# First modulation on unsplit weights in column-tiled pairs, last down pieces and final chain by token halves: a one-core diffusion backbone layer on Trainium2

## The chip, the cores and the metric

The kernel runs on one core of one Trainium2 chip, as one launch. The metric is the device time of that launch in microseconds, from the first to the last instruction of the core and what lies around them. Lower is better.

## What is computed

One layer of a hybrid backbone on 256 tokens `x` and 256 context tokens `ctx`, width 2048, all in fp32. Cut to what matters here:

```python
sh1, sc1, gt1, sh2, sc2, gt2 = adaln(c, w_mod[l], b_mod[l])            # silu(c) @ w_mod + b_mod, 6 rows of 2048
csh1, csc1, cgt1, csh2, csc2, cgt2 = adaln(c_ctx, w_mod[l], b_mod[l])  # of these only csh1 and csc1 are needed
hx = modulate(rms_norm(x, g_mix[l]), sh1, sc1)                         # xn * (1 + scale) + shift
hc = modulate(rms_norm(ctx, g_mix[l]), csh1, csc1)
x_pool, x_u, x_v, x_lru, x_lg, x_q, x_k, x_val = jnp.split(hx @ w_in[l], N_IN_SLICES, axis=-1)
...
x_mixed = x + gt1 * merge_branches(hx, [y_pool, y_sgu, y_lru, y_na], w_branch[l], w_gate[l], w_out[l])
hx2 = modulate(rms_norm(x_mixed, g_ffn[l]), sh2, sc2)
x = x_mixed + gt2 * swiglu(hx2, w_ffn_gate[l], w_ffn_up[l], w_ffn_down[l])
return rms_norm(x, g_final)
```

The "first modulation" is sh1 and sc1, for `c` and for `c_ctx`: two vectors of 2048 against 2048 x 4096 of `w_mod`, 32 MB of weights that are read once. The tokens can't be projected before they are modulated.

## The kernel before

**Pieces.** Every weight matrix comes in pieces of two 128x512 tiles side by side (128x1024 fp32, 512 KB). SyncE issues their transfers into a ring of raw slots. Nearly every piece is split on the chip for two fast matmul passes: ScalarE writes a rounded copy HI (in fp32r), VectorE the rest LO = raw - HI, and TensorE multiplies HI and LO apart. Three matmuls (high by high, high by low, low by high) stand for one in full precision; `rows3` and `piece_rows` (L1276 to L1278) and `piece` issue them. HI and LO have four slots each; ScalarE refills a slot when TensorE has counted the semaphore `used` for the piece that was there. A piece with 256 tokens costs TensorE 12 matmuls of 512 columns, one with 512 tokens (tokens and context) 24.

**The start.** The list `START` has 72 pieces: 64 of the first modulation, as ("mod", q, j), and 8 of the keys' weights, as ("keys", q, j). Quarter q makes 512 columns of shift (j 0 to 7) and of scale (j 8 to 15); j also picks 256 of the 2048 rows. A modulation piece takes four matmuls with the vectors as the stationary operand, 4 columns wide (high and low parts of both vectors, in `SC`), each with HI or LO as its 512 moving columns (L1353). 12 of the 64 pieces, the set `WHOLE`, are left unsplit and take two plain fp32 matmuls with `SCF` (L1347); the chip runs each of these as two instructions. When a quarter is summed up, ScalarE copies its 4 rows out of PSUM (`MROW`, L471), TensorE turns them into columns (`MOD_TURN`, L1244), VectorE adds the bias and makes the factor `A1` (`mod1_columns`), and the four slices of tokens that belong to it are modulated (ScalarE the context, L439; VectorE the tokens, L777) and split into high and low (L446, L782). Then the keys pieces ("keys", q, 0 and 1) can run (`piece`, L1248 to L1250). All of this is one order written by hand: after each piece of `START` each engine runs its `start(p)`. The four rows of tokens and context (`XTOK`, 1 MB each) are sent between the first modulation pieces. Slots of the start are eight (`raw_first`): a raw slot is free when its LO is made, or for an unsplit piece when TensorE has used it.

**The middle** (the other projections, the branches, the gates, the output projection, the feed-forward) is in the same code in both versions. TensorE goes through its pieces in program order; the remaining modulations are summed on VectorE beside it.

**The end.** `ENDING` lists the last 16 pieces of the down projection by column quarter n. Quarter 3 is last: pieces 28 to 31 of the ending, both token halves (PSUM banks 6 and 7) side by side in each piece. `final_down(3)` on VectorE then does 256 tokens in one operation of 128x1024 each: times the gate, plus the residual, times the norm's factor. ScalarE squares and sums, loads the table for the square root, VectorE takes the reciprocal, and both scale the rows, half of the columns at a time, before SyncE stores them in four transfers of 512 KB.

The two lines that say what a modulation piece costs TensorE:

```python
i = mm(ps[0:4, 4 + j // 8, :], SC[:, 2 * (j % 8) + t, :], part[:, p % RING, t * BW:(t + 1) * BW],
       start=j % 8 + t + w == 0, stop=j % 8 + t + w == 9, skip_group_check=True)
```

Of the kernel before, what the change touches and what calls it, by code (L numbers as in the profile page):

```python
# [24 lines left out]
F32R = mybir.dt.float32r  # L25
# [4 lines left out]
P = 128  # L30
D = 2048
# [24 lines left out]
START = [("mod", q, j) for q in range(2) for j in range(16)]  # L56
for _i in range(4):
    START += [("keys", _i // 2, _i % 2)] + [("mod", 2 + _i // 2, _i % 2 * 8 + j) for j in range(8)]
START += [("keys", q, j) for q in (2, 3) for j in range(2)]
STARTED = len(START)  # L60
START_RING = 8

WHOLE = {p for p, (kind, q, j) in enumerate(START) if kind == "mod" and q < 2 and j % 8 in (2, 4, 6)}

MOD_TURN = [23, START.index(("mod", 1, 15)) + 4, START.index(("mod", 2, 15)) + 4, STARTED - 4]

def after_turn(q, steps):

    return STARTED - 1 if q == 3 else MOD_TURN[q] + 3 + steps

WIN0 = STARTED - 8
# [57 lines left out]
def build(nc, x, c, ctx, c_ctx, w_mod, b_mod, g_mix, g_ffn, g_final, w_in, w_pool, pool_scale,  # L133
# [3 lines left out]
    with ctxs:  # L137
# [15 lines left out]
        SC = sb("SC", [P, KT, 4], F32R)  # L153
# [35 lines left out]
        MROW = BR[0:4, 8192:9216]  # L189
        RAWX = BR[:, 10240:12288].rearrange("p (s e) -> p s e", s=2)  # L190
        CROW = BR[0:2 * KT, 12288:12416]
# [34 lines left out]
        def raw_first(p):  # L226
            r = p % START_RING
            extra = (RAWX[:, 0, :], RAWX[:, 1, :], MR.rearrange("p s e -> p (s e)"), ACCM.rearrange("p s e -> p (s e)"))
            return RAW[:, r, :] if r < RING else extra[r - RING]
# [8 lines left out]
        landed_first = [sem(f"first_landed{s}") for s in range(START_RING)]  # L238
# [24 lines left out]
        def _(sp):  # L263
            def first_piece(p, view, q, col):
                last = p - START_RING
                if last in WHOLE:
                    sp.wait_ge(used, last + 1 + 4)
                elif last >= 0:
                    sp.wait_ge(lo_done, last + 1 + 4)
                sp.dma_start(raw_first(p).rearrange("p (t n) -> p t n", t=2),  # L270
                             view[:, q, :, col:col + BW]).then_inc(landed_first[p % START_RING], 16)
# [10 lines left out]
            for p, (kind, q, j) in enumerate(START):  # L282
                if kind == "mod":
                    first_piece(p, v_mod, j % 8, j // 8 * D + q * BW)
                else:
                    first_piece(p, v_in, 2 * q + j, S_K * BW)
                if p in (3, 5, 7, 9):
                    k = (p - 3) // 2
                    sp.dma_start(XTOK[:, k, :], tokens[k]).then_inc(s(f"tokens{k}"), 16)
            for n, sl in enumerate(WIN_ORDER):  # L290
                if n == 0:
                    continue
                for j in range(8):
                    piece(WIN0 + 8 * n + j, j, v_in, j, sl * BW)
# [38 lines left out]
            for half in range(2):  # L333
                for t in range(2):

                    sp.wait_ge(s(f"rows_done{t}"), half + 1)
                    cols = slice(half * D // 2, (half + 1) * D // 2)
                    sp.dma_start(out[0, t * P:(t + 1) * P, cols].rearrange("p (n e) -> p n e", n=2),
                                 OTOK[:, 2 * half:2 * half + 2, t, :]).then_inc(s(f"stored{t}"), 16)
            for t in range(2):  # L340
                sp.wait_ge(s(f"stored{t}"), 32)
# [68 lines left out]
        def _(act):  # L410
            own = Own(act, own_a)

            def first_high(p):

                act.wait_ge(landed_first[p % START_RING], 16 * (p // START_RING + 1))
                act.wait_ge(used, p + 1)
                act.activation(HI[:, p % RING, :], raw_first(p), ACT.Copy).then_inc(hi_done, 2 if p + 1 in WHOLE else 1)  # L417

            def high(base4, j):

                act.wait_ge(landed[j % RING], base4 * 16 + 16 * (j // 4 + 1 - STARTED // RING))
# [7 lines left out]
            act.wait_ge(s("siluc"), 1)  # L429
            act.activation(SC[:, :, 0:2], SCF[:, :, :].rearrange("p w k -> p k w"), ACT.Copy).then_inc(s("sc_hi"), 1)  # L430

            def input_context(q):

                act.wait_ge(s("mod1_ready"), q // 2 + 1)
# [13 lines left out]
            def start(p):  # L448

                if p in (7, 9, 11, 13):  # L450

                    k = (p - 7) // 2
                    act.wait_ge(s(f"tokens{k}"), 16)
                    act.activation(ATT[:, k * D:(k + 1) * D], XTOK[:, k, :], ACT.Square, accum_out=ST[:, k:k + 1])\
                        .then_inc(s("ssq"), 1)
                if p == 13:
                    act.wait_ge(s("ssq"), 4)
                    act.activation(ST[:, 4:8], ST[:, 0:4], ACT.Sqrt, bias=EPSC[:, 0:1], scale=1.0 / D).then_inc(s("rms"), 1)
                if 20 <= p < 28:
                    b = 2 * (p - 20)  # L460
                    act.wait_ge(s("x_turned"), b + 1)
                    act.activation(XT[:, b // 8, b % 4 * 4:b % 4 * 4 + 4, b // 4 % 2 * P:b // 4 % 2 * P + P],
                                   ps[:, b % 4, :].rearrange("p (k t) -> p k t", k=4), ACT.Copy).then_inc(s("xt_act"), 1)
                for q in range(4):
                    for part in range(2):
                        done = START.index(("mod", q, 8 * part + 7))
                        if p == done + 4:
                            act.wait_ge(used, done + 1 + 4)
                            if q:
                                act.wait_ge(s("mod1_turned"), q)  # L470
                            act.activation(MROW[:, part * BW:(part + 1) * BW], ps[0:4, 4 + part, :], ACT.Copy)\  # L471
                                .then_inc(s("mrow"), 1)
                for q in range(4):
                    for t in range(2):
                        if p == after_turn(q, 2 + t):
                            input_context(2 * q + t)
                        if p == after_turn(q, 3 + t):
                            input_high(2 * q + t)

            for p in range(STARTED):  # L480
                if p not in WHOLE:
                    first_high(p)
                start(p)
# [177 lines left out]
            high(FFN0 // 4, 1)  # L661
            square(3)
            act.activation(ST[:, 62:63], EPSC[:, 0:1], ACT.Sqrt)
# [47 lines left out]
            for i in range(8):  # L711
                act.wait_ge(s("xf_new"), i // 2 + 1)
# [15 lines left out]
        def _(dve):  # L728
# [56 lines left out]
            def start(p):  # L785
# [20 lines left out]
                for q in range(4):  # L806
                    if p == after_turn(q, 1):
                        mod1_columns(q)
# [859 lines left out]
```

## Time and profile before

| | |
|---|---|
| median of 3 runs | 1722.19 us (1720.59 to 1722.87) |
| the profiled execution | 1720.87 us |
| its span, first to last instruction | 1719.2 us |
| TensorE busy | 1657.7 us (96%), 7647 matmul instructions |
| VectorE, ScalarE busy | 1150.8 us (67%), 783.6 us (46%) |
| HBM read | 385.30 MB, 226 GB/s over the span |
| mean granted TensorE clock | 0.988 of full speed |

The span is what the rows below are cut from. 1.7 us of the profiled execution lie outside it, and it is 1.3 us below the median. A busy TensorE in the profile is one with an instruction in flight: matmuls overlap, so the distance from start to start says what one costs, not its own length.

### The profile page before, as it was taken

The numbers are of one execution on the slowest core, as the hardware profiler recorded it, in microseconds if no ns is written. First come the engines' busy times: TensorE is split into PE (matmuls) and PEld (weight loads), VectorE is DVE, ScalarE is ACT, GpSimd is POOL, SyncE is SP. The second block draws the span as 40 slices with busy tenths as digits, with TensorE's granted clock in tenths as the row PEclk, the third lists the DMA queues.
The fourth block names the chain that finished last, engine by engine and source line by source line (L and its number), as shares of the span: only waits on it lengthen the run. The fifth ranks groups of instructions, "written<-read, shape, count | busy, mean of one in ns | idle before, by whom it ended". The sixth has DMA issues, their size and how long they took to land.

```text
span 1719.2 us, 22469 instructions
## 1 busy us (share of the span) xinstructions
PE 1657.7 (96%) x7647; PEld 1328.7 (77%) x7647; DVE 1150.8 (67%) x1260; ACT 783.6 (46%) x850; POOL 158.7 (9%) x294
## 2 busy tenths in 40 slices
PE   5899999999989999999999899999999999999996
PEld 1447888897668888878878688888888888888875
DVE  2785345688778888877866658667666555465485
ACT  4584323446764444434444644434444444434433
POOL 1002011110002312313100002011010000000000
PEclk9999999999999999999999899999999999999998
DMA  9887455765448979989855468778786666666552
GB/s 360 290 307 224 123 184 172 232 212 180 135 150 302 326 262 324 338 286 326 289 182 184 128 190 283 235 250 272 236 285 186 193 189 190 188 192 192 161 187 107
DMA packets 183799, 389.10 MB, mean 226 GB/s; under 512 B 14304, under 2 KB 14544, under 8 KB 182848
## 3 DMA queue, kind: packets, MB, share of 16 engines
q1 hardware_dynamic: 160720, 312.63, 56.2%
q0 software_dynamic: 23024, 75.74, 12.8%
q8 instruction: 34, 0.56, 0.1%
q14 instruction: 21, 0.17, 0.0%
HBM read 385.30 MB, written 3.01 MB: 226 GB/s over the span
## 4 chain that ended last, share of the span: by engine, by line
PE 85%; DVE 7%; ACT 4%; DMA 3%; issue 1%; SPq 0%; ACTq 0%; DVEq 0%
PE ps L1276 23%; PE ps L1278 23%; PE ps L1277 23%; PE ps L1248 3%; PE ps L1250 3%; PE ps L1249 3%; DMA RAW<-in_w_mod 2%; PE ps L1244 2%; DVE LO L734 2%; ACT HI L424 1%; DVE LO L738 1%; DMA RAW<-in_w_branch 1%; PE ps L1353 1%; PE ps L1347 1%; ACT HI L417 0%
## 5 line engine op out<-in xcount | busy, mean ns | idle before, releaser
L738 DVE TENSOR_TENSOR LO<-RAW,HI 128x1024 fp32r<-128x1024 f32 x512 | 625.5, 1224 | 459.4 <-ACT HI L424 457.1
L424 ACT ACTIVATE HI<-RAW 128x1024 fp32r<-128x1024 f32 x512 | 541.9, 1060 | 801.9 <-PE ps L1278 679.8
L1276 PE MATMUL ps<-HI,H 128*128 128x512 f32 x1920 | 755.8, 394 | 16.3 <-DVE LO L738 10.8
L1278 PE MATMUL ps<-HI,H 128*128 128x512 f32 x1920 | 749.7, 390 | 0.0
L1277 PE MATMUL ps<-LO,H 128*128 128x512 f32 x1920 | 749.5, 390 | 0.0
L1276 PEld LDWEIGHTS ps<-HI,H 128*128 128x128 f32 x1920 | 361.7, 188 | 97.5 <-DVE LO L738 13.3
L1278 PEld LDWEIGHTS ps<-HI,H 128*128 128x128 f32 x1920 | 361.7, 188 | 75.8
L1277 PEld LDWEIGHTS ps<-LO,H 128*128 128x128 f32 x1920 | 361.9, 188 | 75.1 <-issue 1.2
L388 POOL DMA_DIRECT2D BR<-in_w_mod x208 | 111.8, 538 | 749.8 <-DVE BR L842 330.6
L840 DVE SCALAR_TENSOR_TENSOR BR<-BR,SCF 128x512 f32<-128x512 f32 (+1 forms) x195 | 145.5, 746 | 3.4 <-DMA BR<-in_w_mod 1.9
L1248 PE MATMUL ps<-H,HI 128*128 128x256 f32 (+1 forms) x384 | 123.7, 322 | 3.7 <-DVE LO L734 3.4
L1249 PE MATMUL ps<-H,HI 128*128 128x256 f32 (+1 forms) x384 | 122.3, 319 | 0.0
L1250 PE MATMUL ps<-H,LO 128*128 128x256 f32 (+1 forms) x384 | 122.3, 318 | 0.0
L1248 PEld LDWEIGHTS ps<-H,HI 128*128 128x128 f32 x384 | 73.1, 190 | 11.1 <-issue 6.2
L1250 PEld LDWEIGHTS ps<-H,LO 128*128 128x128 f32 x384 | 73.1, 190 | 5.1
L1249 PEld LDWEIGHTS ps<-H,HI 128*128 128x128 f32 x384 | 73.2, 191 | 4.9
L1353 PE MATMUL ps<-HI,SC 128*4 128x512 f32 x104 | 43.7, 420 | 16.0 <-DVE LO L734 15.5
L734 DVE TENSOR_TENSOR LO<-RAW,HI 128x1024 fp32r<-128x1024 f32 x32 | 38.3, 1221 | 13.9 <-ACT HI L417 13.8
L388 POOL DMA_DIRECT2D MR<-in_w_mod x48 | 26.1, 546 | 210.3 <-DVE ACCM L840 145.7
L1146 DVE TENSOR_TENSOR ATT<-ps,ATT 128x1024 f32<-128x1024 f32 x36 | 43.8, 1216 | 0.0
L1353 PEld LDWEIGHTS ps<-HI,SC 128*4 128x4 f32 x104 | 9.0, 86 | 44.9 <-DVE LO L734 26.5
L1353 PE MATMUL ps<-LO,SC 128*4 128x512 f32 x104 | 43.5, 418 | 0.0
(250 smaller groups left out, 818.8 us busy)
## 6 DMA issues: line engine op xcount, KB each, us to landing
RAW<-in_w_gate SPq DMA_DIRECT2D x128, 512.0 KB, 4.7
BR<-in_w_mod POOLq DMA_DIRECT2D x208, 256.0 KB, 4.5
RAW<-in_w_ffn_gate SPq DMA_DIRECT2D x88, 512.0 KB, 3.8
RAW<-in_w_ffn_up SPq DMA_DIRECT2D x88, 512.0 KB, 3.9
RAW<-in_w_ffn_down SPq DMA_DIRECT2D x88, 512.0 KB, 3.7
RAW<-in_w_in SPq DMA_DIRECT2D x60, 512.0 KB, 4.3
RAW<-in_w_mod SPq DMA_DIRECT2D x32, 512.0 KB, 5.6
RAW<-in_w_branch SPq DMA_DIRECT2D x32, 512.0 KB, 5.0
```

Source lines behind the costliest of these rows:

```text
L388: pool.dma_start(slots[:, k % ring, :], w_mod[0, k * P:(k + 1) * P, bass.ds(2 * D + g * BW, BW)])\
L424: act.activation(HI[:, j % RING, :], RAW[:, j % RING, :], ACT.Copy).then_inc(hi_done, 1)
L734: tt(LO[:, p % RING, :], raw_first(p), HI[:, p % RING, :], ALU.subtract).then_inc(lo_done, 2 if p + 1 in WHOLE else 1)
L738: tt(LO[:, j % RING, :], RAW[:, j % RING, :], HI[:, j % RING, :], ALU.subtract).then_inc(lo_done, 1)
L840: i = stt(acc, src, SCF[:, 0, k:k + 1], acc, ALU.mult, ALU.add)
L1248: mm(o, wh, xh, start=first, stop=False, skip_group_check=True)
L1249: mm(o, wh, xl, start=False, stop=False, skip_group_check=True)
L1250: return mm(o, wl, xh, start=False, stop=last, skip_group_check=True)
L1276: mm(o, xh, wh, start=first and t == 0, stop=False, skip_group_check=True)
L1277: mm(o, xh, wl, start=False, stop=False, skip_group_check=True)
L1278: i = mm(o, xl, wh, start=False, stop=last and t == 1, skip_group_check=True)
L1353: i = mm(ps[0:4, 4 + j // 8, :], SC[:, 2 * (j % 8) + t, :], part[:, p % RING, t * BW:(t + 1) * BW], start=j % 8 + t + w == 0, stop=j % 8 + ...
```

## The change

- **The start.** Modulation pieces are no longer split. `SCP` holds for each 128 rows of `w_mod` the two vectors as plain fp32 columns, padded with zeros to 32. A pair of pieces is four fp32 matmuls, each to its own 32 PSUM partitions (`tile_position=(0, 32 * g)`), that is, in its own quarter of the array's columns; 32 pairs in all (`mod_pair`). The rows to be summed are then at partitions 0, 32, 64 and 96, and `mod1_turn` sums and turns them in one with `PICK`. Scale comes ahead of shift and is turned by itself (`part`). Modulation pieces have 7 raw slots (`MOD_RING`), free when TensorE has used them; keys pieces have raw slots 0 and 1 and are still split (`key_high`, `key_low`). The tokens are sent ahead of all pieces, the keys pieces among the modulation pieces of the same quarter, and TensorE mixes three steps of keys (9 matmuls) behind each of five pairs of the next quarter.
- **The end.** Quarter 3 of the down projection runs its four pieces for tokens 0 to 127 and then again for tokens 128 to 255 (`ending_half`); `last_rows(t)` does the chain for a half of the tokens, each with its own sum, root and reciprocal, and the stores are eight of 256 KB, the first half's ahead. The table for the root is loaded ahead of the last two squares.
- Ahead of the feed-forward, too, the root's table is loaded before the last squares.
- The merge of the branches works in token rows in both versions; no line of it is in the difference.

```diff
-            for p, (kind, q, j) in enumerate(START):
+            for k in range(4):
+                sp.dma_start(XTOK[:, k, :], tokens[k]).then_inc(s(f"tokens{k}"), 16)
+            for kind, q, j in START:
                 if kind == "mod":
-                    first_piece(p, v_mod, j % 8, j // 8 * D + q * BW)
+                    mod_piece(16 * q + j, v_mod, j % 8, (1 - j // 8) * D + q * BW)
                 else:
-                    first_piece(p, v_in, 2 * q + j, S_K * BW)
-                if p in (3, 5, 7, 9):
-                    k = (p - 3) // 2
-                    sp.dma_start(XTOK[:, k, :], tokens[k]).then_inc(s(f"tokens{k}"), 16)
+                    key_piece(2 * q + j)
...
+            def mod_piece(p, view, q, col):
+                if p >= MOD_RING:
+                    sp.wait_ge(s("mod1_used"), p - MOD_RING + 1)
...
+            def mod_pair(q, i):
+
+                part, p = i // 4, 16 * q + 2 * i
+                for p1 in (p, p + 1):
+                    pe.wait_ge(mod1_landed[p1 % MOD_RING], 16 * (p1 // MOD_RING + 1))
+                if q and i % 4 == 0:
+                    pe.wait_ge(s("mrow"), 2 * q - 1 + part)
+                for g in range(4):
+                    k = 4 * (i % 4) + g
+                    m = mm(ps[32 * g:32 * g + 32, 4 + part, :], SCP[:, k, :], mod_raw(p + g // 2)[:, g % 2 * BW:(g % 2 + 1) * BW],
+                           start=i % 4 == 0, stop=i % 4 == 3, skip_group_check=True, tile_position=(0, 32 * g))
+                m.then_inc(s("mod1_used"), 2)
...
+            pe.wait_ge(s("sc_set"), 1)
+            for i in range(8):
+                mod_pair(0, i)
+                if 1 <= i < 5:
+                    for b in range(4):
+                        rows_turn(4 * (i - 1) + b)
...
+            for q in range(1, 4):
+                work = keys(q - 1)
+                for i in range(8):
+                    mod_pair(q, i)
+                    if i == 0:
+                        mod1_turn(q - 1, 1)
+                    if i == 5:
+                        mod1_turn(q, 0)
+                    for _ in range(3 * (2 <= i < 7)):
+                        next(work)
+                next(work)
+            mod1_turn(3, 1)
+            for _ in keys(3):
+                pass
...
+            def ending_half(i, q):
...
+            pe.wait_ge(s("xf_new"), 2)
+            for q in range(2):
+                ending_half(6, q)
+                d = ending_half(7, q)
+                if q == 0:
+                    d.then_inc(s("last_half"), 1)
```

TensorE inside the start, before: the last matmul of a keys piece (L1250) and the first two pieces of modulation behind it.

```order
L1250 MATMUL ps<-H,LO 128x512
L1353 MATMUL ps<-HI,SC 4x512 [waits lo_done,mrow]
L1353 MATMUL ps<-LO,SC 4x512
L1353 MATMUL ps<-HI,SC 4x512
L1353 MATMUL ps<-LO,SC 4x512
L1353 MATMUL ps<-HI,SC 4x512 [waits lo_done]
L1353 MATMUL ps<-LO,SC 4x512
L1353 MATMUL ps<-HI,SC 4x512
L1353 MATMUL ps<-LO,SC 4x512
```

The same place now, in quarter 2: a pair (L1314), three of nine keys matmuls (L1233 to L1235 are `rows3`) and so on in turn.

```order
L1314 MATMUL ps<-BR 32x512 [waits mod1_landed2,mod1_landed1]
L1314 MATMUL ps<-BR 32x512 x3
L1233 MATMUL ps<-H,HI 128x512 [waits lo_done,h_lo]
L1234 MATMUL ps<-H,HI 128x512
L1235 MATMUL ps<-H,LO 128x512
L1233 MATMUL ps<-H,HI 128x512
L1234 MATMUL ps<-H,HI 128x512
L1235 MATMUL ps<-H,LO 128x512
L1233 MATMUL ps<-H,HI 128x512
L1234 MATMUL ps<-H,HI 128x512
L1235 MATMUL ps<-H,LO 128x512
L1314 MATMUL ps<-MR,BR 32x512 [waits mod1_landed4,mod1_landed3]
```

A pair of pieces was eight matmuls that waited for the split (`lo_done`); it is four that wait for the transfers alone, and keys come in between.

SyncE's queue at the start of the program, before (BR, MR and ACCM are raw slots beside RAW; BR<-in_ctx and BR<-in_x are the tokens):

```order
L270 DMA RAW<-in_w_mod 128x2x512 x4
L289 DMA BR<-in_ctx 128x2048
L270 DMA BR<-in_w_mod 128x2x512 x2
L289 DMA BR<-in_ctx 128x2048
L270 DMA MR<-in_w_mod 128x2x512
L270 DMA ACCM<-in_w_mod 128x2x512
L289 DMA BR<-in_x 128x2048
L270 DMA RAW<-in_w_mod 128x2x512 x2
L289 DMA BR<-in_x 128x2048
```

And now:

```order
L278 DMA BR<-in_ctx 128x2048 x2
L278 DMA BR<-in_x 128x2048 x2
L259 DMA BR<-in_w_mod 128x2x512 x3
L259 DMA MR<-in_w_mod 128x2x512
L259 DMA ACCM<-in_w_mod 128x2x512
L259 DMA RAW<-in_w_mod 128x2x512 x2
L259 DMA BR<-in_w_mod 128x2x512 x2
L265 DMA RAW<-in_w_in 128x2x512
```

The 4 MB of tokens moved ahead of the first modulation piece, and the first keys piece (in_w_in) from behind 32 modulation pieces to behind 9.

VectorE at the end of the program, before: `final_down(3)` for all tokens, the sum, the reciprocal, the scaling.

```order
L1193 TENSOR_TENSOR ATT<-ps,ACCM 128x1024 [waits piece_used]
L1194 TENSOR_TENSOR BR<-BR,ATT 128x2x512 [waits dve_own]
L1196 TENSOR_TENSOR ATT<-BR 128x1024 [waits xf_new]
L1226 TENSOR_REDUCE ST<-ST 128x2 [waits sqf]
L1228 MEMSET ST 128x1 [waits dve_own]
L1230 RECIPROCAL ST<-ST 128x2 [waits rms3]
L1235 TENSOR_SCALAR ATT<-ATT,ST 128x2x512 [waits y_new,rstd3]
L1235 TENSOR_SCALAR ATT<-ATT,ST 128x2x512
```

And now, the first of two halves (the second has the same rows, and waits for `piece_used` in place of `last_half`):

```order
L1206 TENSOR_TENSOR ATT<-ps,ACCM 128x512 [waits last_half]
L1207 TENSOR_TENSOR BR<-BR,ATT 128x512 [waits dve_own]
L1209 TENSOR_TENSOR ATT<-BR 128x512 [waits xf_new]
L1211 TENSOR_REDUCE ST<-ST 128x1 [waits sqf]
L1213 RECIPROCAL ST<-ST 128x1 [waits rms3]
L1217 TENSOR_SCALAR ATT<-ATT,ST 128x512 [waits y_new,rstd3]
```

Every operation has half the elements, and the first set waits for TensorE's middle of the last quarter, not for its end.

## Rows read from the trace of the kernel before

**Rows 1.** The page, chain that ended last: shares of the span by engine

```profile
PE 85%; DVE 7%; ACT 4%; DMA 3%; issue 1%; SPq 0%; ACTq 0%; DVEq 0%
```

**Rows 2.** Two stretches: busy of each engine, granted clock, DMA share, GB/s

```profile
10.00:50.00 40.00, 26.77 (x72) 5.98 (x71) 16.60 (x19) 21.29 (x23) 1.13 (x1) 0.88 1.03 388
...
84.90:114.70 29.80, 27.89 (x122) 14.23 (x121) 24.79 (x27) 22.92 (x26) 0.00 (x0) 1.00 0.89 305
```

**Rows 3.** Groups by line and shape, 0 to 150 us: count, busy us, mean ns

```profile
L1353 PE MATMUL ps<-HI,SC 128*4 128x512 f32 x104 | 43.7, 420 | 16.0 <-DVE LO L734 15.5
L734 DVE TENSOR_TENSOR LO<-RAW,HI 128x1024 fp32r<-128x1024 f32 x32 | 38.3, 1221 | 13.9 <-ACT HI L417 13.8
L1347 PE MATMUL ps<-RAW,SCF 128*2 128x512 f32 x16 | 8.1, 629 | 0.0
```

**Rows 4.** Timeline of TensorE in the start: start us, us, engine, line

```profile
51.90 1.03 PE L1244 MATMUL ps<-CST,BR 128*128 128x128 f32 x8
...
144.56 0.65 PE L1244 MATMUL ps<-CST,BR 4*128 4x4 f32 x8
...
145.95 0.39 PE L1248 MATMUL ps<-H,HI 128*128 128x512 f32 x1
...
161.60 0.39 PE L1276 MATMUL ps<-HI,H 128*128 128x512 f32 x1
```

**Rows 5.** The chain that ended last, in the start: start us, us, what

```profile
3.75 7.00 DMA RAW<-in_w_mod
...
52.94 1.81 PE ps L1347 x4
```

**Rows 6.** Groups by line and shape, 140 to 152 us, modulating quarter 3

```profile
L782 DVE TENSOR_TENSOR H<-ATT,H 128x1024 fp32r<-128x1024 f32 x2 | 2.5, 1225 | 1.7 <-ACT H L446 1.7
L439 ACT ACTIVATE ATT<-ATT,MC,A 128x256 f32<-128x256 f32 x4 | 2.2, 591 | 5.5 <-DVE A L766 5.5
L446 ACT ACTIVATE H<-ATT 128x1024 fp32r<-128x1024 f32 x2 | 2.1, 1062 | 0.1
L471 ACT ACTIVATE BR<-ps 4x512 f32<-4x512 f32 x1 | 0.6, 570 | 0.0
L765 DVE TENSOR_TENSOR MC<-ps,MC 128x16 f32<-128x16 f32 x1 | 0.2, 174 | 0.0
```

**Rows 7.** The chain at the first feed-forward piece: start us, us, what

```profile
963.28 1.21 PE ps L1569 x2
...
967.83 0.80 PE ps L1276
...
972.04 0.43 PE ps L1276
```

**Rows 8.** The chain at the end of the program: start us, us, what

```profile
1704.35 0.24 PE ps L1278
...
1704.61 1.24 DVE ATT L1193
...
1707.13 0.73 ACT ATT L715 x2
...
1710.60 1.15 ACT ATT L724
```

**Rows 9.** Timelines of VectorE and ScalarE at the end of the program

```profile
1694.88 1.23 DVE L738 TENSOR_TENSOR LO<-RAW,HI 128x1024 fp32r<-128x1024 f32 x1 [1.49 <-ACT HI L424]
...
1698.54 1.23 DVE L1196 TENSOR_TENSOR ATT<-BR 128x1024 f32<-128x1024 f32 x1
...
1710.60 1.42 DVE L1235 TENSOR_SCALAR ATT<-ATT,ST 128x1024 f32<-128x1024 f32 x2
```

**Rows 10.** Timeline of ScalarE, the root's table

```profile
1708.68 1.28 ACT L717 ACT_TABLE_LOAD   x1
```

**Rows 11.** Groups by line and shape, 940 to 1000 us: 128x512 on VectorE

```profile
L828 DVE TENSOR_TENSOR H<-ATT,H 128x512 fp32r<-128x512 f32 x8 | 5.5, 688 | 1.1 <-ACT H L674 1.1
```

**Rows 12.** Timeline of SyncE's queue: the four stores

```profile
1711.77 3.11 SPq L338 DMA_DIRECT2D out<-ATT  x4
```

More of the change, by code:

```diff
@@ L51 @@
 PITCH = 128
[L56 to L75, printed above, removed]
+START = []
+for _q in range(4):
+    for _j in range(16):
+        if _j in (9, 13):
+            START.append(("keys", _q, _j // 13))
+        START.append(("mod", _q, _j))
+MOD_RING = 7
+WIN0 = 0
 MIX0 = WIN0 + 8 * 8
@@ L480, in _ @@
[L480 to L483, printed above, removed]
+            for k in range(4):
+                act.wait_ge(s(f"tokens{k}"), 16)
+                act.activation(ATT[:, k * D:(k + 1) * D], XTOK[:, k, :], ACT.Square, accum_out=ST[:, k:k + 1])\
+                    .then_inc(s("ssq"), 1)
+            act.wait_ge(s("ssq"), 4)
+            act.activation(ST[:, 4:8], ST[:, 0:4], ACT.Sqrt, bias=EPSC[:, 0:1], scale=1.0 / D).then_inc(s("rms"), 1)
@@ L816, in _ @@
[L816 to L819 removed]
+            dve.wait_ge(s("rms"), 1)
+            own.did(dve.reciprocal(ST[:, 4:8], ST[:, 4:8])); own.wait()
+            for k in range(4):
+                ts(XTOK[:, k, :], XTOK[:, k, :], ST[:, 4 + k:5 + k], None, ALU.mult).then_inc(s("rows_scaled"), 1)
+            for b in range(1, 16, 2):
+                dve.wait_ge(s("x_turned"), b + 1)
+                dve.tensor_copy(XT[:, b // 8, b % 4 * 4:b % 4 * 4 + 4, b // 4 % 2 * P:b // 4 % 2 * P + P],
+                                ps[:, b % 4, :].rearrange("p (k t) -> p k t", k=4)).then_inc(s("xt_dve"), 1)
@@ new lines, in mod1_turn @@
+            def mod1_turn(q, part):
+                pe.wait_ge(s("mrow"), 2 * q + part + 1)
+                pe.wait_ge(s("params"), 1)
+                if q + part:
+                    pe.wait_ge(s("mod1_read"), 2 * q + part)
+                for k in range(4):
+                    c = 64 + 16 * q + 8 * part + 2 * k
+                    m = mm(ps[:, 7, c:c + 2], MROW[:, part * BW + k * P:part * BW + (k + 1) * P], PICK,
+                           start=True, stop=True, skip_group_check=True)
+                m.then_inc(s("mod1_turned"), 1)
@@ L1355, in _ @@
-                i.then_inc(used, 1)
-                start(p)
+                        for f in range(4):
+                            i = rows3(ps[:, f, :], *weights(p, t, f), *both(k0 + t), p + t == 0, p == 7 and t == 1)
+                            if t == 1 and f == 3:
+                                i.then_inc(used, 1)
+                            yield
+            pe.wait_ge(s("sc_set"), 1)
[5 more added lines that the diff above has]
+                if i == 5:
+                    params_turn()
+                if i == 6:
+                    mod1_turn(0, 0)
```

326 lines of the change are left out of this document (150 added, 176 removed).

## The prediction

> **What bounds the kernel now.** I read the chain that ended last first: 85% of it is TensorE [rows 1], so TensorE's program order sets the time, and only its waits or its own matmuls can give any back. Then the busy time by stretches, in the two places that the change touches. In the start there are two regimes. From 10 to 50 us the transfers are at their limit: the 16 DMA engines are full, 388 GB/s, and VectorE is busy for 16.60 of 40 us [rows 2]. After that they are not: from 84.90 to 114.70, one quarter of the start, they move 305 GB/s, TensorE is busy for 27.89 of 29.80 us and VectorE for 24.79, mostly with the splits of 1.22 us each [rows 2, 3]. TensorE comes to the first piece behind the start, the values' weights, at 161.60 us [rows 4]. At the end the reader is to see a serial tail: the last matmul ends at 1704.59 us, and nearly 15 us of VectorE, ScalarE and stores follow, to 1719.2 [rows 8, 12].
>
> **Units.** From the keys matmul at 145.95 to the one at 161.60 there are 69 starts, 0.227 us each [rows 4]. A keys piece has 24, 5.44 us, so the last two take 10.9 us. Two unsplit fp32 matmuls are four instructions in 1.81 us, so 0.905 us for one matmul and 0.4525 us for each of its two instructions [rows 5]. Eight transposed tiles of tokens take 1.0 us, 64 tiles 8 us; a turn of modulation rows takes 0.6 us [rows 4].
>
> **The start, before.** Each split piece of modulation is four matmuls of 0.23 us, 0.92 us; of the 64 pieces 52 are split (104 matmuls with HI, 104 with LO [rows 3]). So modulation costs TensorE 1.84 us for two pieces, and the splits of 52 pieces VectorE 63 us.
>
> **The start, after, by transfers.** 64 modulation and 8 keys pieces are 37.7 MB, the tokens 4.2 MB: 41.9 MB, all of it now queued without a wait for a split. At 388 GB/s [rows 2] that is 108.1 us, and from the first transfer at 3.75 us [rows 5] the last piece is in at 111.9 us. One piece is 1.35 us, a pair 2.70 us.
>
> **The start, after, by TensorE.** The trace has no matmul in a quarter of the columns, so a pair's cost is bounded from both sides. Below: the four matmuls run side by side, a pair in the time of one, 0.905 us. Above: one after another, 3.62 us. To either I add an allowance of 0.1 us for going from one kind of matmul to the other, which I chose. I take the low end: the four have their own columns, weights and PSUM partitions, and use the same rows of nothing but the input, so nothing that I can name in them is shared. What a quarter then costs TensorE: 8 pairs x 1.0 + 16 keys steps x 0.68 + 2 turns x 0.6 = 20.1 us, against 18 pieces x 1.35 = 24.3 us of transfers. The transfers set the pace, and seven raw slots (9.4 us of transfers) cover TensorE's lag, since a pair with nine keys matmuls takes 3.0 us against 2.70.
>
> Here a page of the skill bears on it. The Trainium skill, "TensorE: Matmul & The Clock Gate", Part 3, gives three column tiles of 32 columns and 512 moving columns a speed of 2.38 times one after another. By that, as an estimate, four tiles are some 3.2 times as fast, a pair costs 1.2 us and a quarter 21.7 us, and transfers still set the pace; no row of this case shows a tile.
>
> Behind the last landing at 111.9 us nothing is hidden: the pair 1.0, MROW's copy 0.57, the turn 0.6, the bias 0.17, two context slices 1.1, the high part 1.06, the low part 1.22 [rows 4, 6]: 5.7 us, then the two keys pieces, 10.9 us. In the old kernel this gap was covered by the keys pieces of quarter 2, which now run ahead of it. TensorE waits for some 3.5 us in it. What a wait like this does to the clock the trace shows ahead of the feed-forward: after the work at 963.28 (1.21 us) TensorE waits until 967.83, and the 11 matmuls from there to the one at 972.04 take 0.43 us each, the 1.2 GHz level, where the rest runs at 2.4 [rows 7]. That costs 11 x 0.2 = 2.2 us; I count it in full. So the values' weights start at 111.9 + 5.7 + 10.9 + 2.2 = 130.7 us where they started at 161.60: **30.9 us less**.
>
> What could spoil this in the first quarter: the tokens come first, so the first pair lands at 3.75 + 10 x 1.35 = 17.3 us, and TensorE idles until then. It has 8 pairs and 64 transposes to do in the first quarter, 16 us at the low price, while 16 pieces take 22 us, so it keeps up even at a clock of 0.88 [rows 2]. The squares, the root and the scaling of the tokens on ScalarE and VectorE lie in the same stretch, where neither has a split to do.
>
> **The middle.** The same instructions in the same order, fed through the same four slots: shifted, not changed. The table load that goes ahead of the last squares before the feed-forward takes 1.28 us [rows 10] off ScalarE's chain, but VectorE's copy of the last turned columns runs beside it there and ends as late. 0 us.
>
> **The end.** 48 matmuls of the last quarter stay 48. A half needs all four split pieces within 4 x 1.36 us. The last split ran from 1694.88 to 1696.1 [rows 9], the quarter starts at 1704.59 - 10.88 = 1693.7, and the half wants piece four at 1697.8: in time by 1.7 us. Tokens 0 to 127 are through at 1699.2. VectorE is at `final_down(2)` until 1699.8 [rows 9] and then does the first half's chain, three operations of 0.69 us [rows 11] and about 2.5 us more, by 1704.3, beside TensorE. At 1704.59 the second half: two operations of 0.69, the square 0.73 [rows 8], sum, root and reciprocal. These took 1710.60 - 1708.68 = 1.9 us with the table's 1.28 [rows 8, 10], so 0.66 without (the load starts when the squares end). One scaling, 0.4 us where 1024 columns take 0.71 [rows 9]. First store of the second half: 1704.59 + 1.40 + 0.73 + 0.66 + 0.4 = 1707.8, against 1711.77 [rows 12]. From that issue to the end it was 7.4 us for 2.10 MB, which at 388 GB/s is 5.4 us and 2.0 us fixed; for 1.05 MB it is 4.7. End at 1712.5: **6.7 us less**.
>
> **The sum.** 1719.2 - 30.9 - 6.7 = 1681.6 us span; the profiled execution lies 1.7 us above its span and the median 1.3 us above that: 1684.6 us. A measurement tells 0.2%, 3.4 us, from no change.
>
> **Rivals.**
>
 Against it: nothing. A quarter then costs TensorE 18.9 + 10.9 + 1.2 = 31.0 us and not the transfers' 24.3. The first quarter ends at 17.3 + 18.9 + 8 = 44.2, the fourth at 137.2, the start at 137.2 + 4.7 + 10.9 + 2.2 = 155.0: 6.6 us less. With the end's 6.7: 1705.9 span, 1709 us.
>
> *One after another* (the other side). A pair costs 3.72 us, a quarter 41.9 us. The first quarter ends at 17.3 + 29.8 + 8 = 55.1, the fourth at 180.8, the start at 198.6, which is 37 us later; with the end's 6.7 less, 1749.5 span, 1752 us. The start ends at 17.3 + 8 + 3 x 12.1 + 4.7 + 10.9 + 2.2 = 79.4 us plus 32 pairs, so it breaks even at a pair of 2.57 us and the whole kernel, with the end's 6.7 us, at 2.78; from there on it is slower. For it: no row shows any two matmuls side by side. Changing the array's tiling may also make TensorE run empty first, as the Trainium skill has it in "TensorEngine Tiling (Array Packing)", Key Properties; 0.2 us in each of 32 pairs would be 6 us where TensorE sets the pace.
>
> *Transfers don't hold the rate.* 388 GB/s is a row of 40 us. At 350 the start is 11.7 us longer, 1696 us.
>
> *The change does nothing* where the start gains what the clock and the gap behind the last landing take: needs a pair of 2.7 to 2.9 us, within 0.1 us of the break-even point.
>
> **Chances.** Side by side 0.53 (with a slower transfer rate in it 0.08), by halves 0.27, one after another or over 2.9 us a pair 0.16, in between with no change 0.04. The range leaves out the last two: from 1677 (400 GB/s, clock not lowered) to 1713 (by halves with 4 us of emptying). Faster 0.80, same 0.04, slower 0.16.
>
> **What the next profile shows.** If right: starts of the pair's eight instructions in some 0.9 us, about 388 GB/s without a gap until 112 us, the values' first matmul near 131 us, the stores of the first half ahead of TensorE's end, and 8 us from TensorE's last matmul to the end of the span. Wrong: a pair's starts spread over 2.3 or 3.6 us; a GB/s below 350 from 50 us on, with SyncE waiting for used slots; a wait of VectorE for the last table load.

## The result, and the profile after

The changed kernel takes **1693.27 us** (median, 1691.66 to 1694.98) beside 1721.39 (1720.51 to 1722.87) for the kernel before, measured with it: ratio 0.9837, 95% interval 0.9824 to 0.9849. Measured again (e0 below) it took 1692.87 beside 1721.70, ratio 0.9828 (0.9815 to 0.9842). That is 28.1 us less; 37.6 were forecast from 1722.19 us, and 1693.3 lies in the range, 8.7 us above the forecast. The profiled execution has a span of 1690.5 us, against 1719.2 before, and lies 1.65 us above it.

The chain of the page, which answers to [rows 1]: TensorE's share went from 85 to 87%, so it is still its program order that counts, and the modulation's matmuls (L1314) stand on it with 1%.

```profile
PE 87%; DVE 5%; ACT 3%; DMA 3%; issue 1%; SPq 0%; DVEq 0%; ACTq 0%
```

Busy time by stretches (us, then busy us of each engine with the count, the granted clock, the DMA share, GB/s), answering to [rows 2]:

```profile
10.00:50.00 40.00, 24.73 (x154) 12.82 (x154) 13.75 (x20) 15.46 (x20) 1.13 (x1) 0.91 1.04 386
50.00:100.00 50.00, 48.11 (x265) 24.47 (x265) 14.41 (x26) 15.64 (x22) 0.00 (x0) 0.94 1.04 378
101.70:120.30 18.60, 18.38 (x102) 9.98 (x102) 4.81 (x6) 4.39 (x6) 0.00 (x0) 1.00 0.94 338
120.30:139.40 19.10, 15.37 (x64) 12.41 (x61) 7.60 (x15) 7.74 (x10) 11.23 (x17) 0.82 0.72 235
```

The reader sees three regimes. Up to 100 us the transfers are near their limit and VectorE is busy for 28 of 90 us: the splits of the modulation are gone. From 101.7 to 120.3 TensorE is busy for 18.38 of 18.60 us and the rate falls to 338 GB/s, so there TensorE sets the pace. Behind it the clock is at 0.82 on average and TensorE idle for 3.7 us. The timeline of TensorE (start, us, line, operands, idle before) at the third pair of quarter 3, which is called (3,2) below since both are counted from 0, at the pairs behind it, at the last pair, and at the values' first matmul, which answers to 161.60 in [rows 4]:

```profile
101.70 0.62 PE L1314 MATMUL ps<-MR,BR 128*32 128x512 f32 x2 [1.63 <-DMA ACCM<-in_w_mod]
101.72 0.62 PE L1314 MATMUL ps<-ACCM,BR 128*32 128x512 f32 x2
102.13 0.62 PE L1314 MATMUL ps<-MR,BR 128*32 128x512 f32 x2
102.17 0.60 PE L1314 MATMUL ps<-ACCM,BR 128*32 128x512 f32 x2
102.70 0.50 PE L1233 MATMUL ps<-H,HI 128*128 128x512 f32 x1
103.03 0.39 PE L1234 MATMUL ps<-H,HI 128*128 128x512 f32 x1
103.27 0.40 PE L1235 MATMUL ps<-H,LO 128*128 128x512 f32 x1
...
104.65 0.39 PE L1235 MATMUL ps<-H,LO 128*128 128x512 f32 x1
104.97 1.06 PE L1314 MATMUL ps<-RAW,BR 128*32 128x512 f32 x8
105.96 0.50 PE L1233 MATMUL ps<-H,HI 128*128 128x512 f32 x1
...
108.52 1.06 PE L1314 MATMUL ps<-BR 128*32 128x512 f32 x8 [0.21 <-issue]
...
119.73 0.60 PE L1314 MATMUL ps<-BR 128*32 128x512 f32 x2
120.26 0.50 PE L1233 MATMUL ps<-H,HI 128*128 128x512 f32 x1
120.59 0.39 PE L1234 MATMUL ps<-H,HI 128*128 128x512 f32 x1
120.83 0.40 PE L1235 MATMUL ps<-H,LO 128*128 128x512 f32 x1
121.06 1.04 PE L1326 MATMUL ps<-BR 128*128 128x2 f32 x8
125.83 0.80 PE L1233 MATMUL ps<-H,HI 128*128 128x512 f32 x1 [3.73 <-DVE H L768]
126.42 0.63 PE L1234 MATMUL ps<-H,HI 128*128 128x512 f32 x1
...
139.36 0.39 PE L1261 MATMUL ps<-HI,H 128*128 128x512 f32 x1
```

Four things are read from it. A pair's eight instructions start in two groups of four, each within 0.04 us, the second 0.43 to 0.45 us behind the first: the four matmuls do run side by side, and from a pair's start to the keys behind it are 0.99 us (104.97 to 105.96). The keys matmul next to a pair costs more than the 0.23 us of the others: 0.32 us from its start to the pair's (104.65 to 104.97), and 0.33 for the first one behind a pair (102.70 to 103.03). From the first matmul behind the last pair, 120.26, to the keys of quarter 3 are 5.57 us, of which TensorE waits for 3.73. And the first matmul after that wait lasts 0.80 us and the next 0.63 where the others last 0.39; twelve of them start some 0.43 us apart, at a granted clock of 0.50 from 125.83 to 131.11: the 1.2 GHz level. The values' first matmul is at 139.36, **22.2 us** ahead of before.

The end, as the chain that ended last shows it (start, us, engine, line), which answers to [rows 8]:

```profile
1682.50 0.70 DVE ATT L1206
1683.21 0.02 issue
1683.23 0.70 DVE BR L1207
1683.93 0.02 issue
1683.95 0.73 ACT ATT L700 x2
1684.68 0.02 issue
1684.71 0.17 DVE ST L1211
1684.88 0.02 issue
1684.90 0.30 ACT ST L704
1685.20 0.02 issue
1685.23 0.17 DVE ST L1213
1685.40 0.03 issue
1685.43 0.49 DVE ATT L1217
```

TensorE's last matmul ends at 1682.48 and the span at 1690.5: 8.0 us behind it where there were 14.6, **6.6 us** less. SyncE's queue has the first of the eight stores at 1681.37, ahead of TensorE's end:

```profile
1681.37 6.37 SPq L337 DMA_DIRECT2D out<-ATT  x8
```

Between the values' first matmul and TensorE's end nothing moved: 1542.99 us before, 1543.12 after. So 22.2 + 6.6 - 0.1 = 28.7 us, which is the difference of the two spans.

### The profile page after: what moved, and what is told of

The parts are those of the page before. It is cut to its first block, busy times and chain, and to the rows that moved or that the text cites. A ratio compares the mean times of both kernels' runs of the same rounds, so it can differ in the third digit from the quotient of the medians.

```text
span 1690.5 us, 22406 instructions
## 1 busy us (share of the span) xinstructions
PE 1630.3 (96%) x7679; PEld 1322.8 (78%) x7679; DVE 1094.8 (65%) x1218; ACT 733.3 (43%) x798; POOL 159.2 (9%) x294
## 4 chain that ended last, share of the span: by engine, by line
PE 87%; DVE 5%; ACT 3%; DMA 3%; issue 1%; SPq 0%; DVEq 0%; ACTq 0%
PE ps L1261 24%; PE ps L1263 23%; PE ps L1262 23%; PE ps L1233 4%; PE ps L1234 4%; PE ps L1235 4%; PE ps L1229 2%; PE ps L1314 1%; ACT HI L422 1%; DMA BR<-in_w_mod 1%; DVE LO L722 1%; DMA MR<-in_w_mod 1%; DMA RAW<-in_w_branch 1%; PE ps L1398 0%; PE ps L1412 0%
## 5 line engine op out<-in xcount | busy, mean ns | idle before, releaser
L722 DVE TENSOR_TENSOR LO<-RAW,HI 128x1024 fp32r<-128x1024 f32 x512 | 625.7, 1224 | 458.7 <-ACT HI L422 456.3
L1233 PE MATMUL ps<-H,HI 128*128 128x256 f32 (+1 forms) x384 | 126.9, 330 | 5.5 <-DVE H L768 5.4
L1234 PE MATMUL ps<-H,HI 128*128 128x256 f32 (+1 forms) x384 | 123.7, 322 | 0.0
L1235 PE MATMUL ps<-H,LO 128*128 128x256 f32 (+1 forms) x384 | 123.6, 322 | 0.0
L1233 PEld LDWEIGHTS ps<-H,HI 128*128 128x128 f32 x384 | 74.0, 193 | 23.9 <-issue 10.1
L1235 PEld LDWEIGHTS ps<-H,LO 128*128 128x128 f32 x384 | 74.0, 193 | 5.5
L1314 PE MATMUL ps<-BR 128*32 128x512 f32 x112 | 24.4, 716 | 17.0 <-DMA BR<-in_w_mod 13.7
L814 DVE SCALAR_TENSOR_TENSOR ACCM<-MR,SCF,ACCM 128x512 f32<-128x512 f32 x45 | 33.6, 748 | 8.6 <-DMA MR<-in_w_mod 8.6
L1229 PEld LDWEIGHTS ps<-CST,BR 128*128 128x128 f32 (+1 forms) x173 | 21.1, 148 | 12.9 <-DMA CST<-in_cst 4.0
```

Source lines behind the costliest of these rows:

```text
L722: tt(LO[:, j % RING, :], RAW[:, j % RING, :], HI[:, j % RING, :], ALU.subtract).then_inc(lo_done, 1)
L814: i = stt(acc, src, SCF[:, 0, k:k + 1], acc, ALU.mult, ALU.add)
L1229: return mm(o, src, IDENT[0:n, 0:n], start=start, stop=True, is_transpose=True, skip_group_check=True)
L1233: mm(o, wh, xh, start=first, stop=False, skip_group_check=True)
L1234: mm(o, wh, xl, start=False, stop=False, skip_group_check=True)
L1235: return mm(o, wl, xh, start=False, stop=last, skip_group_check=True)
```

## The experiments

Ten runs in three groups: e1, e2, e3 and e5; e0, e4, e6 and e8; e9 and e10. Each group was measured together with the kernel before (medians 1722.12, 1721.70 and 1720.93 us), and a difference is taken inside a group, or by the ratio to its own before.

**Start and end apart.** The start of the changed kernel with the old end and the old places of the table loads, and the other way round; the diffs are the two halves of the one above.

> The new start with the old end and the old place of the root's table loads. My theory: the start's gain (the values' first matmul at 139.4 us where it was at 161.6) reaches the end whole, and start and end add up: 22 us less than the kernel before, 0.987 of its time. Rival: part of the start's gain is lost or doubled in the middle and the sum of the two parts is off by more than 3 us: then this run is not between 0.985 and 0.989.

> The old start with the new end (and both table loads moved). My theory: 6.6 us less than before, 0.996 of its time, with 8.0 us from TensorE's last matmul to the end of the span where it was 14.6. Rival: the halves cost TensorE something at the end or the table load ahead of the feed-forward gives something too: then the time from the values' first matmul to TensorE's last is off 1543.0 us by more than 1 us.

Start alone: 1698.82 us, ratio 0.987 (0.9854 to 0.9887), 23.3 us less; the values' first matmul is at 138.19 and the tail still 14.6 us long. End alone: 1713.36, ratio 0.9951 (0.9935 to 0.9968), 8.8 us less. Its tail is 8.0 us, so 6.6 of the 8.8 are the end's; by the traces 1.3 us more lie in the old start, whose first matmul of the values came at 160.26 and not at 161.60, with its code unchanged. By the traces, then, 22 to 23 us are the start's and 6.6 the end's, and neither shows in the other's place. The medians can't show it as finely: their differences add up to 32.1 us where both changes together gave 28.1, and each of the two is known to some 3 us.

**One column tile.** The four matmuls of a pair in the same quarter of the columns, and summed there (cut; ScalarE's copy and the turning then take 32 partitions):

```diff
-                    m = mm(ps[32 * g:32 * g + 32, 4 + part, :], SCP[:, k, :], mod_raw(p + g // 2)[:, g % 2 * BW:(g % 2 + 1) * BW],
-                           start=i % 4 == 0, stop=i % 4 == 3, skip_group_check=True, tile_position=(0, 32 * g))
+                    m = mm(ps[0:32, 4 + part, :], SCP[:, k, :], mod_raw(p + g // 2)[:, g % 2 * BW:(g % 2 + 1) * BW],
+                           start=i % 4 + g == 0, stop=i % 4 == 3 and g == 3, skip_group_check=True, tile_position=(0, 0))
```

> The changed kernel with the four matmuls of each pair in the same column tile and the same 32 partitions, one after another; the same result. My theory, that side by side is what makes unsplit weights pay: a pair takes 3.6 us in place of 1.0, TensorE sets the pace of the start, a quarter takes 8 x 3.7 + 12.1 = 42 us, the values' first matmul comes near 200 us, the span is near 1750 us. Rival, that the array runs fp32 matmuls of 32 columns faster in any case, or that the transfers hide them: the span stays under 1700 us.

1757.08 us (one run), 35 us slower than before, with a span of 1755.4. Its TensorE timeline and its stretches:

```profile
150.31 1.88 PE L1314 MATMUL ps<-MR,BR 128*32 128x512 f32 x4
152.02 1.88 PE L1314 MATMUL ps<-ACCM,BR 128*32 128x512 f32 x4
153.83 0.50 PE L1233 MATMUL ps<-H,HI 128*128 128x512 f32 x1
```

```profile
10.00:50.00 40.00, 31.57 (x116) 12.47 (x117) 10.99 (x15) 14.74 (x19) 1.13 (x1) 1.00 0.87 318
50.00:190.00 140.00, 136.27 (x417) 54.59 (x415) 25.59 (x44) 26.23 (x37) 0.00 (x0) 1.00 0.65 214
```

A pair takes 3.52 us here (150.31 to 153.83) and 0.99 in four tiles, the transfers fall to 214 GB/s, and TensorE comes to the values at 203.5 us. This is the first theory, and its numbers were near 200 and 1750 us. Unsplit weights in one tile make this kernel slower than it was before the change; that the four tiles run side by side is what the start lives on.

**Keys held back.** Against the forecast 8.7 us are missing, and three things could make them up: the landings of the pieces, TensorE's work, and the gap behind the last pair with its low clock. Here nine of quarter 2's sixteen keys steps stand behind the last pair in place of one, two ahead of the last turning and seven in the gap behind it:

```diff
-                    for _ in range(3 * (2 <= i < 7)):
+                    for _ in range((1 if q == 3 and i > 2 else 3) * (2 <= i < 7)):
                         next(work)
-                next(work)
+                if q < 3:
+                    next(work)
+            next(work)
+            next(work)
             mod1_turn(3, 1)
+            for _ in work:
+                pass
```

> The changed kernel, with 8 of the 16 steps of the keys of quarter 2 moved from between the pairs of quarter 3 to behind its last pair, 7 of them behind the last turn. Theory: the wait of 3.7 us behind the last turn and the slow clock after it (the first 11 matmuls of the last keys at 0.43 us) are what an order with nothing left to do makes; TensorE also reaches the last pair earlier, since in quarter 3 it and no longer the transfers sets the pace (18.6 us from the pair at 101.7 to the end of the last). Then the values' first matmul comes at 133 to 135 us, the kernel is 4 to 6 us faster than the changed one, 0.980 to 0.982 of the kernel before. Rival: the last pair is bound by its transfers' landing and comes no earlier; then only the wait is filled, and it is 2 to 4 us faster; if the clock falls all the same, 0 to 2 us.

1690.37 us, ratio 0.9817 (0.98 to 0.9833), against 0.9837 and 0.9828 for the changed kernel: some 2 to 3 us less, with intervals that overlap. That is what the rival said (2 to 4 us), not the theory's 4 to 6. Three of its last four pairs:

```profile
107.89 1.06 PE L1314 MATMUL ps<-BR 128*32 128x512 f32 x8 [1.55 <-issue]
...
114.58 0.62 PE L1314 MATMUL ps<-ACCM,BR 128*32 128x512 f32 x2 [1.22 <-DMA RAW<-in_w_mod]
...
117.33 0.62 PE L1314 MATMUL ps<-RAW,BR 128*32 128x512 f32 x2 [0.80 <-DMA BR<-in_w_mod]
```

The last two now wait for their pieces. So does the first, though the profile puts its wait down to "issue": by the trace's landing events (the semaphore's count when a transfer is complete) its second piece landed at 107.80, 0.09 us ahead of it. The clock is at 1.00 from 120 to 130 us, no wait for the modulated tokens (H) is left, and the values start at 136.38, 3.0 us sooner. But the last pair came only 1.9 us sooner, from 119.26 to 117.33, and then it was the landings that held it.

**What holds the landings.** Four kernels measured together. The first, e0, is the changed kernel itself. In e4 POOL writes its 0.9 MB of bias tables (`toeplitz_rows`, from SBUF to HBM) only when all modulation pieces are used; in e6 keys come five steps behind every second pair; e8 is e4 with held keys: nine steps between the pairs, one behind the last pair and six behind the last turning (its expectation says seven). The edits of e4, of e6, and what e8 adds to e4's (cut):

```diff
             pool.wait_ge(s("rp_in"), 16 * NB)
+            pool.wait_ge(s("mod1_used"), 64)
```

```diff
-                    for _ in range(3 * (2 <= i < 7)):
+                    for _ in range({2: 5, 4: 5, 6: 5}.get(i, 0)):
```

```diff
-                    for _ in range(3 * (2 <= i < 7)):
+                    for _ in range((3, 3, 1, 1, 1)[i - 2] if 2 <= i < 7 and q == 3 else 3 * (2 <= i < 7)):
                         next(work)
```

> The changed kernel itself, unaltered, timed beside the three next ones. 1693.3 us is its first median; 1692 to 1695 expected, with the values' first matmul near 139.4 us.

> POOL's 0.9 MB of bias tables are asked for only when all 64 modulation pieces are used, instead of among them. Theory A (pieces landing set the pace of the start up to 101.7 us, as the wait of 1.63 us for the pair there shows): at the 381 GB/s of 3 to 110 us the 0.9 MB are 2.4 us; the landings move by that, TensorE keeps 1.6 to 2.4 of it, median 1690.9 to 1691.7 us. Theory B (TensorE's own work and its changes of tiling pace the start from 57 us on, and the 1.63 us would only be waited elsewhere): under 0.7 us, 1692.6 or more.

> The keys' steps between two modulation pairs stand as five behind every second pair in place of three behind each of five: three groups instead of five in each quarter, so two changes each way fewer per quarter. If a change of tiling costs TensorE some 0.5 us both ways (0.37 ahead of a pair, 0.12 behind it), the last quarter, paced by TensorE from 101.7 us on, ends 1.0 us sooner: 1692.3 us, and two pairs in a row show no gap of their own between them. If the landings pace the last quarter too, the pairs wait for their transfers in place of the change, and nothing moves (within 0.3 us); the groups of five could also put a pair's slot free later, and cost some tenths.

> The bias tables late as in e4, and the keys of quarter 2 held back as in e5, with one step ahead of the last turning in place of two and seven behind it. In e5 the last pair waited 0.80 us for its piece, so there the landings bound the end of the modulation; without the 0.9 MB they come 2.4 us sooner. If that is so, the last pair ends near 116 us and not 118.3, the values' first matmul starts near 134.5 and not 136.4, and the median falls to about 1688.5 us. If TensorE's own work is what is left (the sum of its matmuls, no idle time), it stays at e5's 1690.4 within 0.5 us.

| | median, range (us) | ratio to before | last pair starts | values start |
|---|---|---|---|---|
| e0 | 1692.87 (1690.37 to 1694.04) | 0.9828 (0.9815 to 0.9842) | 121.10 | 140.25 |
| e4 | 1689.95 (1687.85 to 1695.35) | 0.9819 (0.9803 to 0.9835) | 117.12 | 136.84 |
| e6 | 1692.59 (1690.79 to 1694.00) | 0.9827 (0.9813 to 0.9840) | 122.16 | 141.75 |
| e8 | 1686.37 (1684.32 to 1688.25) | 0.9794 (0.9780 to 0.9807) | 114.08 | 131.84 |

The last two columns are of one trace each, and e0's carry a stretch of low clock: from 100 to 105 us it was granted 0.53, and pair (3,3) followed (3,2) by 6.0 us in place of 3.27. Pair (3,2) in e0 and in e4:

```profile
101.16 1.07 PE L1314 MATMUL ps<-MR,BR 128*32 128x512 f32 x2 [1.65 <-DMA ACCM<-in_w_mod]
```

```profile
99.61 0.62 PE L1315 MATMUL ps<-MR,BR 128*32 128x512 f32 x2 [1.63 <-DMA ACCM<-in_w_mod]
```

The bias tables do cost. The median of e4, 2.9 us lower than e0's, doesn't show it alone, since the ratios' intervals overlap. The landings do, e6 with its other order left aside: in the five traces with the tables among the pieces (the first profile, e0, e1, e5, e10) the last piece of pair (3,2) landed at 100.7 to 101.6 us and the last of all at 116.8 to 117.6; in the three without (e4, e8, e9) at 97.6 to 99.5 and 113.7 to 115.5. That is 2.8 us in the mean of either, where 0.9 MB are 2.4.

Changes of tiling cost less than I took: my 0.5 us was read off pair (3,4), at 108.52, which had waited for its piece; over most groups it is 0.1 ahead and 0.1 behind, and two fewer each way in the last quarter are 0.4 us, which e0 and e6 can't tell apart. In e6, besides, the second pair of two in the last quarter waited, 0.27 us in one place and 0.46 in the other.

e8 has late tables and held keys: 6.5 us less than e0, intervals apart. Its TensorE at the last two pairs, and the stretches behind them:

```profile
111.53 0.62 PE L1315 MATMUL ps<-ACCM,BR 128*32 128x512 f32 x2 [1.23 <-DMA RAW<-in_w_mod]
...
114.08 0.62 PE L1315 MATMUL ps<-RAW,BR 128*32 128x512 f32 x2 [0.58 <-DMA BR<-in_w_mod]
```

```profile
120.00:130.00 10.00, 10.00 (x45) 8.27 (x45) 5.42 (x10) 4.33 (x5) 7.01 (x11) 1.00 0.88 262
130.00:140.00 10.00, 10.00 (x46) 8.26 (x44) 2.45 (x2) 3.89 (x3) 4.34 (x7) 1.00 1.04 317
```

TensorE has no idle time from 120 to 140 us and a clock of 1.00; the last pair is 5.2 us sooner than in the first profile. This was 2 us more than I had expected.

**Even steps.** The first profile of the changed kernel has a dip in its transfers, where nine keys matmuls and a pair (3.27 us) take longer than two pieces (2.70):

```profile
70.00:75.00 5.00, 5.00 (x36) 2.42 (x39) 0.00 (x0) 0.60 (x1) 0.00 (x0) 1.00 0.97 308
```

So the keys of quarters 0 and 1 were spread two steps behind each pair, on top of e8 (e9, with ten steps of quarter 2 ahead of the last turning and six behind it, just as e8 has; its expectation counts one as moved, which was not) and alone (e10). The edit is e9's, cut; in e10 the row for quarter 3 is (2, 2, 3, 3, 3, 3, 3, 1).

```diff
+            steps = {1: (0, 0, 2, 2, 2, 2, 2, 2), 2: (2, 2, 2, 2, 2, 2, 2, 2), 3: (2, 2, 2, 2, 2, 2, 1, 1)}
+            work = (None for q in range(3) for _ in keys(q))
             for q in range(1, 4):
-                work = keys(q - 1)
...
-                    for _ in range(3 * (2 <= i < 7)):
+                    for _ in range(steps[q][i]):
```

> All that e8 has, and the keys' steps of quarters 0 and 1 spread evenly, two behind each pair, the last four behind the next quarter's first two pairs, in place of three behind each of five pairs; of quarter 2 ten stand ahead of the last turning and six behind it. In the changed kernel the pairs of 57 to 73 us are 3.3 us apart, TensorE's own work, while two pieces arrive in 2.7 us, and the transfers fall to 308 GB/s from 70 to 75 us. If that is a loss of the start's pace, the last landings come 1.0 to 1.3 us sooner than in e8, and the held step moved ahead of the last pair's wait gives 0.7 more: near 1684.5 us. If not (what TensorE loses there it gets back in its waits of 1.3 and 1.65 us near 73 and 98 us), it stays at e8's 1686.4 within 0.7 us.

> The even spread of quarters 0 and 1 alone, on the changed kernel, with quarter 2 three behind each pair as before and the bias tables where they were. If TensorE's uneven load is what delays the landings of the last quarter, pair (3,2), which started at 101.7 us after a wait of 1.63 us for its piece, comes 1.0 to 1.3 us sooner, and the median is near 1691.7 us; no stretch of 5 us from 20 to 100 us is below 370 GB/s. If the landings have other causes, (3,2) stays at 101 to 102 us and the median at 1692.9.

e9: 1685.21 us (1682.97 to 1685.62), ratio 0.979 (0.9776 to 0.9803). e10: 1690.99 (1689.46 to 1691.56), ratio 0.9822 (0.9808 to 0.9835). Neither differs from e8 and e0 by more than the intervals. In e9 no 5 us between 20 and 110 fell below 385 GB/s, yet the last pair started at 113.88 beside e8's 114.08. But e8 had 363 GB/s from 70 to 75 us and e0 373: most of the 308 was of that one execution, so e9 took away a small dip and tells nothing of a deep one. In e10 the dip only moved:

```profile
45.00:50.00 5.00, 5.00 (x32) 1.35 (x24) 3.05 (x6) 0.96 (x2) 0.00 (x0) 0.68 1.02 356
50.00:55.00 5.00, 3.51 (x15) 1.29 (x12) 3.32 (x6) 3.83 (x6) 0.00 (x0) 0.66 0.98 351
```

and pair (3,2) stood at 101.96 with no wait, since the steps left over from quarter 1 now lie ahead of it on TensorE; the last pair, at 119.18, was where the first profile had it (119.26). The last piece of (3,2) landed at 101.22, inside the 100.7 to 101.6 of the four others with the tables among the pieces. Its median is nearer to the 1691.7 us of the dip theory than to 1692.9, but its ratio can't be told from either earlier one of the changed kernel. A gain from even steps isn't shown. e9 has the lowest median of the versions tried, with e8 within its interval: some 36 us faster than before, where the change as given is 28 to 29.

## Why the prediction was right, and where its sum was off

**Mechanism.** Right: four tiles run side by side, and the pair lasts 0.99 us where 1.0 was taken, and 3.52 in one tile, where the bound from above was 3.62. That 0.99 and 1.0 agree is in part luck: 0.1 of the 1.0 was for the change of kind, which costs 0.2 on top of the 0.99 (below). The rival by halves is dead: the second instruction of one tile didn't hold back the first of the next. The Trainium skill's rule that matmuls start and end in program order ("TensorE: Matmul & The Clock Gate", Part 3), from which I had drawn 2.26 us, is not what the trace shows if the two instructions of an fp32 matmul stand next to each other; the trace can't tell in which order they reach the array, but only that four start within 0.04 us. The same page's 2.38 for three tiles, as an estimate 3.2 times for four, was too low: here it is 3.6 times (3.52 against 0.99).

**The end.** 6.7 us were forecast and 6.6 measured, by the same steps. The first half's stores left ahead of TensorE's end, as it said, and the table load was through by 1679.27, ahead of it too.

**The middle.** 0 forecast, 0.1 measured.

**The start.** 30.9 us forecast, 22.2 measured: 8.7 short. The mechanism held; the time of the landings, TensorE's work in the last quarter and the chain behind the last pair with its slow keys were each put too low.

- *The landings: 6.1 us.* Pair (3,2) needs 68 pieces with the tokens; at 1.35 us from 3.75 that is 95.6, and it started at 101.70, after waiting for its piece. The queues up to then (packets, MB, share of the 16 engines), with POOL's write:

```profile
DMA packets 18183, 37.61 MB, mean 370 GB/s; under 512 B 1455, under 2 KB 1695, under 8 KB 17666
...
q1 hardware_dynamic: 17489, 36.53, 97.6%
q0 software_dynamic: 688, 1.01, 3.0%
...
toeplitz_rows<-ATT POOLq DMA_DIRECT2D x1, 896.0 KB, 10.3
```

  And POOL's queue in the kernel before, in the stretch of [rows 2] from 10 to 50 us, of 15.53 MB in all:

```profile
q0 software_dynamic: 424, 0.92, 6.7%
```

  68 pieces are 35.65 MB, and 37.61 had been moved. 1.01 MB were POOL's, nearly all bias tables: 2.6 us at 388 GB/s. The same write was part of the 388 GB/s that the prediction read, and was left out of the bytes that it added up. Another 0.88 MB, 2.3 us, are SyncE's constants and parts of the next pieces: six more were asked for by then, and a piece took some 8 us from request to landing. That leaves 1.2 us for a rate below 388. The first of these is shown by the landings of e4, e8 and e9. The second is worked out from the bytes, and e9 agrees: without tables or dip the last piece of (3,2) landed at 97.64, 2.1 us behind 95.6, and 0.84 MB beyond the 68 pieces had then been moved on SyncE's queue.
- *TensorE behind (3,2): 1.3 us.* The prediction let the transfers set the pace to the end, 16.3 us and a pair. From 101.70 to 120.26 it was mostly TensorE, 18.56 us: five groups of 3.27 us where 3.05 were reckoned, because a change of tiling costs 0.1 us on either side of a pair beside the pair's own 0.99; a turning of 0.92 and not 0.6; and 0.28 us of waiting at (3,4), whose second piece landed at 108.43, 0.09 us ahead of its start. The profile calls this wait "issue", as it does the 1.55 us of the same pair in e5. e5 and e8 show both sides: less work there, and the pairs wait for pieces again. The last piece landed at 117.64, 1.6 us ahead of the last pair at 119.26: the two limits stand that near to each other, so that taking one away gave only part of its price.
- *The chain behind the last pair: 0.9 us*, 5.57 against 4.7: the turning starts 0.80 us behind the pair where 0.57 was reckoned for the copy ahead of it (the copy ends at 120.99, so the three keys matmuls in between cost 0.07 at most), takes 1.04 and not 0.6, and what follows takes 3.73 and not 3.55. *The last keys at a low clock: 0.4 us*, 13.53 against 13.1. That the gap lowers the clock, taken from the rows ahead of the feed-forward [rows 7], was right. e5 and e8 filled it, and the clock stayed up.

6.1 + 1.3 + 0.9 + 0.4 = 8.7 us. The rival of a lower transfer rate was the nearest to what happened (350 GB/s, 1696 us), but the rate hardly fell: 378 to 386 GB/s up to 100 us. It was what was moved that had been undercounted.

What stays open: with bias tables and dip gone, e9's last piece lands at 113.74 where 111.9 was reckoned. The rate there falls to 250 GB/s from 110 to 115 us. SyncE asks for the last modulation piece at 105.62 and for nothing more until 112.20, since its next request waits until VectorE has split the last keys piece; so the last pieces are alone under way. Whether other requests or another order there would bring the last landing forward wasn't tried.

## What to carry to other kernels

A reckoning by transfers has to list every byte on the queues up to the point of the wait, other engines' requests and pieces in flight too, and not only the stream that is watched: 2 MB of 37.6 were 5 us here. When a change takes the splits away and makes transfers the limit, look next at requests in that stretch that nobody waits for yet (0.9 MB put off: landings 2.8 us sooner). And keep independent work back for the dependent chain behind the last landing: here it covered the gap and the clock stayed up. Neither was clear of noise by itself in the medians; the two together were, with 6.5 us.

## What was unexpected of the hardware

Four fp32 matmuls in their own 32 columns, 512 moving columns each, cost hardly more than one, 0.99 us against 0.905, although each is two instructions. Going between 128 and 32 columns costs 0.1 us each way. The 16 DMA engines held 386 GB/s from 20 to 110 us without a break (e9). And the clock differs between executions of one kernel in the same place: from 100 to 120 us it was 1.00 in the first profile of the changed kernel and 0.83 in the second, and in the second the last pair came 1.8 us later though its pair (3,2) was 0.5 us sooner. Landings differ too: up to pair (3,2) e4 and e8 are the same program, and its last piece landed at 99.48 in one and at 97.85 in the other. A single timeline is good to some 2 us there.
